# Value products of a streaming attention: both value parts in one stationary operand, one channel summed on GpSimd, loads spread

## What is computed

```python
logits = jnp.einsum('bqhd,bkhd->bhqk', qblk, k, preferred_element_type=jnp.float32) * scale
logits = logits + cblk.swapaxes(1, 2)[..., None] - ck_t[:, :, None, :]
mask = k_pos[None, :] <= pblk[:, None]
logits = jnp.where(mask, logits, -jnp.inf)
probs = jax.nn.softmax(logits, axis=-1)
return jnp.einsum('bhqk,bkhd->bqhd', probs.astype(v.dtype), v)
```

## Time and profile before

| | us |
|---|---|
| median of three runs | 1908.87 |
| profiled execution | 1905.99 |
| its span | 1904.0 |
| prompt attention, from and to (timeline) | 1063 to 1474 |
| TensorE busy in the span | 1860.6 (98%) |
| VectorE busy | 1293.6 (68%) |
| ScalarE busy | 854.4 (45%) |
| GpSimd busy | 186.0 (10%) |

### The profile page before, as it was taken

The page is one execution under the profiler, slowest core; times in us unless marked ns, Lnnn a source line. Parts: engine busy times, 40 slices in busy tenths (PEclk is TensorE's granted clock), DMA queues, the critical chain, the costliest instruction groups (busy, mean ns, idle before and its releaser), DMA issues.

```text
span 1904.0 us, 28724 instructions
## 1 busy us (share of the span) xinstructions
PE 1860.6 (98%) x10604; PEld 1722.6 (90%) x10604; DVE 1293.6 (68%) x2255; ACT 854.4 (45%) x1594; POOL 186.0 (10%) x153
## 2 busy tenths in 40 slices
PE   7999999999999999999999899999999899999998
PEld 6999999999999999999999787788788799998885
DVE  8879787944545365444656688888996734457887
ACT  5555556634343443433323577777778700111000
POOL 1000000000000000000000202333333500000111
PEclk9999999999999999999999999999999999999999
DMA  6898898969788886879887816566654797765441
GB/s 223 281 327 285 296 332 284 321 228 328 266 305 305 277 305 212 301 234 325 265 299 242 204 28 122 127 134 134 134 104 144 229 375 238 243 183 162 137 147 72
DMA packets 272782, 435.99 MB, mean 229 GB/s; under 512 B 63252, under 2 KB 139188, under 8 KB 268508
## 3 DMA queue, kind: packets, MB, share of 16 engines
q1 hardware_dynamic: 266884, 425.64, 71.0%
q10 hardware_dynamic: 5760, 8.52, 1.2%
HBM read 285.18 MB, written 148.78 MB: 228 GB/s over the span
## 4 chain that ended last, share of the span: by engine, by line
PE 81%; DVE 9%; DMA 3%; SPq 3%; issue 2%; ACT 2%; POOLq 0%; POOL 0%; DVEq 0%; ACTq 0%
PE fr_b L639 4%; PE fr_b L640 4%; PE fr_b L641 4%; PE fr_c L639 4%; PE fr_c L640 4%; PE fr_c L641 4%; PE fr_a L640 4%; PE fr_a L641 4%; PE fr_a L639 4%; PE ln_b L2548 3%; PE ln_b L2550 3%; PE ln_b L2549 3%; PE at_o L1692 3%; PE at_m L1708 3%; PE at_s L1675 3%; PE at_s L1676 3%
## 5 line engine op out<-in xcount | busy, mean ns | idle before, releaser
L817 ACT ACTIVATE fr_wq<-fr_raw 128x512 fp32r<-128x512 f32 x288 | 178.2, 628 | 210.4 <-PE fr_d L641 136.9
L1785 DVE TENSOR_TENSOR at_p_lo<-at_s,at_p_hi 128x512 fp32r<-128x512 f32 (+1 forms) x320 | 192.0, 603 | 42.5 <-ACT at_s L1755 41.0
L1754 ACT ACTIVATE at_p_hi<-at_s 128x512 fp32r<-128x512 f32 (+1 forms) x320 | 169.9, 531 | 83.9 <-PE at_s L1676 49.7
L1108 DVE TENSOR_TENSOR fr_wq<-fr_raw,fr_wq 128x512 fp32r<-128x512 f32 x288 | 192.4, 684 | 10.6 <-ACT fr_wq L817 7.3
L639 PE MATMUL fr_b<-fr_xh,fr_wq 128*128 128x348 f32 x568 | 185.3, 326 | 7.8 <-DVE fr_wq L1108 4.7
L639 PE MATMUL fr_c<-fr_xh,fr_wq 128*128 128x348 f32 x568 | 183.8, 324 | 0.5 <-DMA fr_wq<-w_mixed 0.5
L639 PE MATMUL fr_a<-fr_xh,fr_wq 128*128 128x348 f32 x568 | 183.5, 323 | 0.0
L641 PE MATMUL fr_b<-fr_xh,fr_wq 128*128 128x348 f32 x568 | 183.2, 323 | 0.0
L640 PE MATMUL fr_a<-fr_xl,fr_wq 128*128 128x348 f32 x568 | 183.1, 322 | 0.0
L640 PE MATMUL fr_b<-fr_xl,fr_wq 128*128 128x348 f32 x568 | 183.0, 322 | 0.0
L640 PE MATMUL fr_c<-fr_xl,fr_wq 128*128 128x348 f32 x568 | 182.7, 322 | 0.0
(11 more groups left out here) (390 smaller groups left out, 4679.0 us busy)
## 6 DMA issues: line engine op xcount, KB each, us to landing
fr_wq<-w_mixed SPq DMA_DIRECT2D x192, 512.0 KB, 5.5
fr_raw<-w_tiles SPq DMA_DIRECT2D x96, 512.0 KB, 5.3
...
```

Of the source, the lines that this page charges most:

```text
L817: act.activation(wh[:, idx], operand(i, idx), ACT.Copy).then_inc(w_hi[idx], 1)
L1108: dve.tensor_tensor(wl[:, idx], operand(i, idx), wh[:, idx].bitcast(F32), ALU.subtract).then_inc(w_lo[idx], 1)
L1754: act.activation(p_hi[:, r, cols], s_bank[r][:, cols], ACT.Exp, scale=SCALE)
L1785: dve.tensor_tensor(p_lo[:, r, cols], s_bank[r][:, cols], p_hi[:, r, cols].bitcast(F32), ALU.subtract)\
```

## The change

High and low values of a block lie side by side in one stationary operand, `v_both`: 64 high channels, 64 low. Two matmuls (`p_hi`, `p_lo`) give the high sums in rows 0 to 63 of the bank and the low sums in rows 64 to 127. The place of the low part's first channel holds ones instead, so row 64 is the sum of the probabilities. The low part of that first channel goes another way. In most steps it is a third matmul with `v_first`, a stationary operand that is zero but for its first column. In every second step off the diagonal (kb odd, `pooled`: 12 of 40 in a head), GpSimd does it: it scales `p_hi` by the channel's value for each key (`tensor_scalar`, 128x512) and adds it into one of two accumulators by turns (`tensor_tensor`), 12 scalings and 9 additions a head. One closing matmul a group (`close`, groups 1 to 3) sums the accumulator over the keys into row 0.

ScalarE now copies the bank's lower half to `part` (`copy_part`), and VectorE's `take` adds that to the upper half, with a factor that is 0 for the row of sums. ScalarE also waits, before it refills a slot of `p_hi`, for GpSimd's scaling of it. The round trip of the sums is cut in four, one a group, with `invert`, `scale`, `gate`, `upper` and `lower` at new steps, some in the same head. SP's queue is written anew: the loads for the next head are spread one by one between the small transfers, the values load first, the gate's load comes after the sums of group 0, and the loads of the sample's keys are spread over head 7. In the front the low values of head 0 are loaded right after the high ones.

```diff
-        v_hi, v_lo = (main[:, :, 2 + x].rearrange("p a (b c) -> p a b c", c=P) for x in range(2))
+        v_both, v_first = (main[:, :, 2 + x].rearrange("p a (b c) -> p a b c", c=P) for x in range(2))
+        first_row = sb("first_row", [P, P], 29184, F32R)
+        acc = [sb(f"acc{i}", [P, QW], (29312, 29832)[i], F32R) for i in range(2)]
+        lanes = sb("lanes", [P, 1], 29824)
+        part = sb("part", [P, 2 * NQ, QW], 34880)
...
-        INVERT = 9
-        FINISH = {20 + 4 * q + x + x // 2: (q, x) for x in range(3) for q in range(NQ)}
-        FINISH_LOW = {st + 5: q for st, (q, x) in FINISH.items() if x == 0}
+        INVERT = {16: (0, 0), 23: (0, 1), 33: (0, 2), 13: (1, 3)}
+        SCALE_AT = {22: (0, 0), 38: (0, 1), 0: (1, 2), 20: (1, 3)}
+        GATE_AT = {23: (0, 0), 39: (0, 1), 1: (1, 2), 21: (1, 3)}
+        UPPER_AT = {30: (0, 0), 4: (1, 1), 6: (1, 2), 28: (1, 3)}
+        LOWER_AT = {37: (0, 0), 9: (1, 1), 10: (1, 2), 36: (1, 3)}
+        V_AT = 11
+        PART_AT = {(e + 5) % NS: (0 if e + 5 < NS else 1, q) for q, e in enumerate(ends)}
+        TAKE_AT = {(e + 4) % NS: (0 if e + 4 < NS else 1, q) for q, e in enumerate(ends)}
         TURN = 32
+
+        def pooled(st):
+            q, kb = steps[st]
+            return kb < 4 * q and kb % 2 == 1
...
         def sum_store(sp, h, q):
-            sp.wait_ge(o_read, NQ * h + q + 3)
-            sp.dma_start(s["sums"][h:h + 1, q * QW:(q + 1) * QW], y[HD:HD + 1, h % 2, q * QW:(q + 1) * QW])\
+            sp.wait_ge(part_done, NQ * h + q + 1)
+            sp.dma_start(s["sums"][h:h + 1, q * QW:(q + 1) * QW], part[HD:HD + 1, (NQ * h + q) % (2 * NQ), :])\
               .then_inc(sum_out, 16)
...
+            def load_ahead(h, n):
+                if h + 1 < H:
+                    load_main(h + 1, n)
+                else:
+                    sam.key_load(sp, n)
...
+                if h + 1 < H:
+                    load_values(h + 1)
+                if h == 1:
+                    sam.early_loads(sp)
                 if h:
                     sum_store(sp, h - 1, 3)
-                    sums_load(sp, h - 1)
-                    rcp_store(sp, h - 1)
-                    rcp_load(sp, h - 1)
-                sp.dma_start(zb[:, h % 2], s["zb"][h * HD:(h + 1) * HD, 0:SEQ]).then_inc(zb_in[h % 2], 16)
-                if h + 1 < H:
-                    if h:
-                        sp.wait_ge(pv_done, NS * h + RING)
-                    load_main(h + 1)
-                if h + 2 < H:
-                    if h == 0:
-                        sp.wait_ge(ones_set, 2)
-                    load_max(h + 2)
-                if h == 1:
-                    sam.early_loads(sp)
-                if h == H - 1:
-                    sam.key_loads(sp)
+                    sums_load(sp, h - 1, 3)
+                load_ahead(h, 0)
                 sum_store(sp, h, 0)
-                sum_store(sp, h, 1)
-                if h:
-                    y_store(sp, h - 1, 0)
-                sum_store(sp, h, 2)
                 if h:
                     y_store(sp, h - 1, 1)
+                sums_load(sp, h, 0)
+                load_gate(h)
+                load_ahead(h, 1)
+                if h:
+                    y_store(sp, h - 1, 2)
+                    rcp_store(sp, h - 1, 3)
+                    rcp_load(sp, h - 1, 3)
+                load_ahead(h, 2)
+                rcp_store(sp, h, 0)
+                sum_store(sp, h, 1)
+                rcp_load(sp, h, 0)
+                sums_load(sp, h, 1)
+                load_ahead(h, 3)
+                rcp_store(sp, h, 1)
+                load_max(h + 2, 0)
+                rcp_load(sp, h, 1)
+                load_max(h + 2, 1)
+                sum_store(sp, h, 2)
+                load_max(h + 2, 2)
+                sums_load(sp, h, 2)
+                rcp_store(sp, h, 2)
                 if h + 1 < H:
                     max_rows(sp, h + 1)
+                rcp_load(sp, h, 2)
                 if h:
-                    y_store(sp, h - 1, 2)
                     y_store(sp, h - 1, 3)
+                if h < H - 1:
+                    y_store(sp, h, 0)
...
-                pe.matmul(o, v_hi[:, b, kb, :], p_hi[:, r, cols], start=(kb == 0), stop=False)
-                pe.matmul(o, v_hi[:, b, kb, :], p_lo[:, r, cols], start=False, stop=False)
-                pe.matmul(o, v_lo[:, b, kb, :], p_hi[:, r, cols], start=False, stop=(kb == 4 * q + 3))\
-                  .then_inc(pv_done, 1)
+                pe.matmul(o, v_both[:, b, kb, :], p_hi[:, r, cols], start=(kb == 0), stop=False)
+                last = pe.matmul(o, v_both[:, b, kb, :], p_lo[:, r, cols], start=False, stop=False)
+                if not pooled(st):
+                    last = pe.matmul(o, v_first[:, b, kb, :], p_hi[:, r, cols], start=False, stop=(q == 0 and kb == 3))
+                last.then_inc(pv_done, 1)
+
+            def close(h, q):
+                if h == 0 and q == 1:
+                    pe.wait_ge(first_row_set, 2)
+                pe.wait_ge(acc_done, added_through(h, q))
+                pe.matmul(o_bank[q % 2][:, :], first_row[:, :], acc[(3 * h + q - 1) % 2][:, :], start=False, stop=True).then_inc(closed, 1)
...
+                    if h and st == 0:
+                        close(h - 1, NQ - 1)
+                    if st - 1 in ends[1:-1]:
+                        close(h, ends.index(st - 1))
...
+                before = (h, st - RING) if st >= RING else (h - 1, st - RING + NS)
+                if before[0] >= 0 and pooled(before[1]):
+                    act.wait_ge(acc_scaled, pooled_through(*before))
                 act.activation(p_hi[:, r, cols], s_bank[r][:, cols], ACT.Exp, scale=SCALE)
                 act.activation(s_bank[r][:, cols], s_bank[r][:, cols], ACT.Exp, scale=SCALE).then_inc(p_done, 1)
+
+            def copy_part(h, q):
+                n = NQ * h + q
+                if q:
+                    act.wait_ge(closed, 3 * h + q)
+                else:
+                    act.wait_ge(pv_done, NS * h + ends[q] + 1 + RING)
+                if n >= 2 * NQ:
+                    act.wait_ge(sum_out, 16 * (n - 2 * NQ + 1))
+                    act.wait_ge(o_read, n - 2 * NQ + 3)
+                act.activation(part[HD:2 * HD, n % (2 * NQ), :], o_bank[q % 2][HD:2 * HD, :], ACT.Copy).then_inc(part_done, 1)
...
             def take(h, b, q):
-                dve.wait_ge(pv_done, NS * h + ends[q] + 1 + RING)
+                dve.wait_ge(part_done, NQ * h + q + 1)
                 if h > 1:
                     dve.wait_ge(yl_done, NQ * (h - 1))
-                dve.tensor_copy(y[:, b, q * QW:(q + 1) * QW], o_bank[q % 2][0:HD + 1, :]).then_inc(o_read, 1)
+                o = o_bank[q % 2]
+                dve.scalar_tensor_tensor(out=y[0:HD, b, q * QW:(q + 1) * QW], in0=part[HD:2 * HD, (NQ * h + q) % (2 * NQ), :], scalar=lanes[HD:2 * HD, :],
+                                         in1=o[0:HD, :], op0=ALU.mult, op1=ALU.add).then_inc(o_read, 1)
...
+                    job = at_step(TAKE_AT, h, st)
+                    if job:
+                        take(job[0], job[0] % 2, job[1])
+                    if at_step(INVERT, h, st):
+                        invert(dve, *at_step(INVERT, h, st))
...
+            def free_first_channel(h):
+                b = h % 2
+                if h:
+                    pool.wait_ge(v_in[b], used(h, 2, 32))
+                else:
+                    pool.wait_ge(lead.v_in, 32)
+                pool.tensor_copy(v_first[:, b, :, 0:1], v_both[:, b, :, HD:HD + 1].bitcast(F32)).then_inc(v_ready, 1)
+                pool.wait_ge(v_ready, 2 * h + 1)
+                pool.memset(v_both[:, b, :, HD:HD + 1].bitcast(F32), 1.0).then_inc(v_ready, 1)
...
+            def first_channel(h, st):
+                q, kb = steps[st]
+                r, n, c = st % RING, pooled_through(h, st), 3 * h + q - 1
+                own = v_first[:, h % 2, kb, 0:1].bitcast(F32)
+                this, other = acc[c % 2], acc[(c + 1) % 2]
+                added = n - c - 1
+                pool.wait_ge(p_done, NS * h + st + 1)
+                if kb == 1:
+                    if c:
+                        pool.wait_ge(acc_done, added)
+                    pool.tensor_scalar(this[:, :], p_hi[:, r, :].bitcast(F32), own, None, ALU.mult).then_inc(acc_scaled, 1)
+                else:
+                    if kb == 3 and c:
+                        pool.wait_ge(closed, c)
+                    if added > 1:
+                        pool.wait_ge(acc_done, added - 1)
+                    pool.tensor_scalar(other[:, :], p_hi[:, r, :].bitcast(F32), own, None, ALU.mult).then_inc(acc_scaled, 1)
+                    pool.wait_ge(acc_scaled, n)
+                    pool.tensor_tensor(this[:, :], this[:, :].bitcast(F32), other[:, :].bitcast(F32), ALU.add).then_inc(acc_done, 1)
```

175 lines of the change are left out of this document (104 added, 71 removed).

## The result

The changed kernel takes 1931.11 us (median of 5 runs, 1928.13 to 1933.2), the kernel before 1906.26 us beside it: ratio 1.0124, 95% interval 1.0112 to 1.0137. It is slower by 1.2%, and lies outside my range of 1891 to 1914 around 1903.1 us. The profiled execution has a span of 1930.1 us, 26.1 more than before.

A forecast was written before the change was run, and what follows sets the result against it. TensorE and VectorE were taken as both nearly full up to step 32. Heads 0 to 6 -5.6, head 7 -1.5, single places +1.2, -0.8, +0.9: -5.8 us, 1903.1 us from the median 1908.87; range 1891 to 1914.

The forecast's parts named there:

- What bounds the kernel: Up to step 32 of head 3 VectorE is nearly as full as TensorE; at most about 2.4 us could be squeezed out.
- Head 7: Last head, no maxima to make: TensorE -2.1 us, but ScalarE gets four copies for one less; -1.5 (-2.1 to 0).
- Steps 0 to 11: Each of heads 0 to 6: step 4 starts late for `take`, most made up by step 12; +0.2 us (-0.2 to +0.6).
- Steps 12 to 23: Each of heads 0 to 6: TensorE -0.70 us, VectorE idles 0.59 to some 0.9; -0.6 us (-0.2 to -0.7).
- Steps 24 to 31: Each of heads 0 to 6: TensorE -0.70 us, VectorE idles 0.07, 0.24 with hidden parts; -0.2 us (0 to -0.7).
- GpSimd's port holds VectorE at the turn: Rival, chance 0.16: busy GpSimd holds VectorE's small operations through group 3, +0.8 us a head, about 1908.7 us.
- Steps 32 to 39: Each of heads 0 to 6: a `y_hi` copy moves away, but next scores wait for `qm` stores; -0.2 us (0 to -0.5).
- the sums come late to VectorE: Rival, chance 0.10: sums' round trips share a queue with large loads; 1 us waits at three in seven heads, 1924 us.
- both signs that I had named for the slow side: Signs the forecast is wrong on the slow side: a scaling of 1.5 us or more, or VectorE waiting for `sums`.
- that rival: "GpSimd becomes the bound", chance 0.12: ScalarE's `p_hi` refills wait for scalings over 1.2 us; at 1.9 us, 1930 us.
- All of TensorE's gain arrives: Rival, chance 0.28: VectorE's gaps close and the late step 4 is made up wholly; -15.5 us, 1893 us.
- Single places: One-off costs: library load in head 0 +1.2 us (0 to 3), start -0.8 (0 to -2), end +0.9.

The follow-up runs named there:

- e4: Kernel before, with the third value product left out in 12 steps a head and nothing in its place: 1900.73 us, ratio 0.9965.
- e11: e4 with VectorE's four copies a head out of the bank also given to ScalarE: 1892.56 us, ratio 0.9932.
- e13: e9 with VectorE's additions at the steps of the old copies and each closing product right behind its group's last step: 1918.76 us, ratio 1.0063.
- e14: e13 with a VectorE copy in the addition's place, so the low products don't reach the output: 1909.28 us, ratio 1.0015.
- e16: Changed kernel, low half's copy written to partitions 0 to 63, one buffer for it, closing products 32 channels wide and ahead of the last step: 1924.99 us.
- e9: Changed kernel with the edits of e5, e6 and e7 together, and head 7 without GpSimd's sums: 1914.9 us, ratio 1.0049.
- e17: e9 with e16's copies and closing products: 1906.50 us, ratio 1.0002.
- e5: Changed kernel with steps 29 and 31 of every head not given to GpSimd, keeping their third product: 1930.45 us, ratio 1.0127.
- e1: Changed kernel without GpSimd's sums: every step keeps its third product, closing matmuls gone: 1926.07 us, ratio 1.0095.
- e6: Changed kernel with the last group closed at its end, its copy and addition two steps earlier in the next head: 1930.32 us, ratio 1.0116.
- e7: Changed kernel with head 7's inversions of groups 0 to 2, with their stores and loads, moved behind the head: 1932.12 us, ratio 1.0123.

## Why the prediction was wrong, step by step

In heads 3 to 6 I forecast 0.8 us less each, and they take 2.3 to 2.4 more; in head 7 I forecast 1.5 less, and it takes 8.7 more. Two steps carry this: that a VectorE as full as TensorE would let most of the saved products through and make up the late step 4, and that the transfers were covered in head 7 too.

**What bounds the kernel** was right in kind: both engines are full up to step 32. e4 and e11 put a number on it. Head 7 shows the other side: without maxima its steps 12 to 24 fell from 12.95 to 12.25 us, the whole 0.70 of TensorE.

**Steps 0 to 11.** That step 4 starts late for `take` held (1.11 us of wait against my 1.1 to 1.3). The step that failed is "most is made up by step 12, since VectorE's total hardly changes: the new `take` has 512 columns as the old": +1.6 us came of +0.2, and steps 4 to 12, which were to make it up, took 11.11 us for 11.06. VectorE's total does change, as the addition holds it for 0.95 and not 0.61, four times a head. I took one length for another without asking for the distance to the next start. e13 to e14 shows 1.4 us a head for the addition. e16 shows 1.7, of which four holds shorter by 0.29 are at most 1.2; the rest goes with its other edits. In steps 0 to 12 the place weighs more than the hold: e9, with the addition still held, has 1.2 of the 1.6 us back, and e17 the other 0.4.

**Steps 12 to 23.** Forecast -0.6, measured +0.5. The addition's hold is 0.34 of it and the three inversions 0.08 each, and in e16 these steps are 16.48. But the forecast was wrong without them too: in e4, with nothing added to VectorE, the 0.70 of TensorE gives 0.18, and in e14, with a copy for the addition, 0.25. I had let it into VectorE's idle 0.59 to 0.9 us, and it doesn't fit there.

**Steps 24 to 31.** Forecast -0.2, measured +1.0 in heads 3 to 6: the mechanism of the rival "GpSimd's port holds VectorE at the turn" came true, with 1.16 to 1.28 us for an operation of 0.17 us, while heads 1 and 2 escaped it. Its price of 0.8 us a head didn't: steps 24 to 40 together are 0.3 to 0.4 longer than before, and e5, without the hold, is no faster. **Steps 32 to 39**: forecast -0.2, measured -0.7, part of it that hold given back.

**Head 7** failed most: -1.5 forecast, +8.7 measured. The mechanism is that of my rival "the sums come late to VectorE", which I placed in head 1 and priced at 1 us a time; in head 1 VectorE waited 0.7 us, and in head 7 once 8.0 us. What failed is the cover: I had counted it for the loads of keys, queries and values within head 3, and put the sample's 1 MB key loads, which share head 7's queue with the round trips, at nothing. TensorE waited 6.79 us for it, and while it did the granted clock fell to the lower of its two levels (1.2 GHz), window of after:

```profile
1476.10:1482.90 6.80, 3.44 (x8) 2.77 (x9) 3.50 (x7) 1.08 (x2) 3.32 (x4) 0.50 0.62 196
```

**GpSimd.** A scaling was forecast at 1.0 us, between 0.48 and 1.29; it is 1.56, outside the bounds (group of after, GpSimd).

```profile
L1995 POOL TENSOR_SCALAR at_acc<-at_p_hi,at_main 128x512 fp32r<-128x512 f32 x72 | 112.6, 1564 | 27.7 <-ACT at_s L1825 21.7 <-POOL at_acc L1997 6.0
```

With VectorE's wait for the sums, both signs that I had named for the slow side came. The point from which I had GpSimd decide (a scaling over 1.2 us) was passed, and yet e1 shows 5 us for all that its sums do: that rival fell although its condition held. I read it as the ring of four slots and the steps without a pair giving cover in heads 0 to 6; no run separates this. GpSimd's lateness does decide in head 7, of 41 us (e9), and behind e6's gain. The Trainium skill (GPSIMD Engine Reference, section 3.1) gives 0.77 us for 512 elements as its best case; the 1.564 us here are twice that.

**Counts and rivals.** The page has 72 matmuls fewer, 96 products less 24 closing ones, as forecast. "All of TensorE's gain arrives" is refuted by e4, where a quarter of it does in heads 3 to 6 with nothing else changed.

**Single places.** I had put 1.2 us for a library load in head 0. The trace shows none: the first scaling waits for ScalarE alone, and steps 4 to 12 of head 0 are 11.04 us in after and 11.06 in e1, where GpSimd has no scaling.

```profile
1069.64 1.57 POOL L1989 TENSOR_SCALAR at_acc<-at_p_hi,at_main 128x512 fp32r<-128x512 f32 x1 [1.12 <-ACT at_s L1825]
```

The 5.28 us of the earlier trace rows, from which I took the bound, were a wait for VectorE, as the row says. The attention starts 3.6 us earlier (forecast 0.8), but among the profiles whose start is as in after it lies at 1063.9 to 1069.8, and at 1065.2 to 1068.2 in those with the old start, so that this is not shown as the change's. What follows the attention took 4.1 us more (forecast 0.9): 1.1 in the sample part and 3.3 in the merge, with 0.3 less behind it; the merge took 183.7 to 189.2 us among kernels that have the same one. I leave it open. That also keeps e7 from being read to the last us.
